# One projection of a split-precision decoder layer: both parts of h in one product, two PSUM pairs

## What is computed

```python
def even_mixer(h, w_in, lb, hg_norm_g, ret_norm_g, w_out):
    p = (h @ w_in).astype(jnp.float32)
    ...
    hq, hf, hi, hgate, rq, rk, rv, rgate = jnp.split(p, splits, axis=-1)
    f = lb + (1.0 - lb) * jax.nn.sigmoid(hf)
    o_hg = from_chunks(hgrn2_scan(to_chunks(jax.nn.silu(hq), HG_HEADS), to_chunks(1.0 - f, HG_HEADS),
                                  to_chunks(jnp.log(f), HG_HEADS), to_chunks(hi, HG_HEADS)))
```

## Time and profile before

| | |
|---|---|
| median of three executions | 895.02 us |
| the profiled execution | 895.32 us |
| its span (first to last instruction) | 893.5 us |
| outside the span | 1.8 us |
| TensorE busy | 884.4 us, 99% |
| VectorE busy | 652.2 us, 73% |
| ScalarE busy | 498.4 us, 56% |
| weights read | 159.73 MB on the SyncE queue |

### The profile page before, as it was taken

The page is one execution under the profiler, slowest core; times in us unless marked ns, Lnnn a source line. Parts: engine busy times, 40 slices in busy tenths (PEclk is TensorE's granted clock), DMA queues, the critical chain, the costliest instruction groups (busy, mean ns, idle before and its releaser), DMA issues.

```text
span 893.5 us, 13339 instructions
## 1 busy us (share of the span) xinstructions
PE 884.4 (99%) x5610; PEld 756.6 (85%) x5610; DVE 652.2 (73%) x790; ACT 498.4 (56%) x676; POOL 31.1 (3%) x25
## 2 busy tenths in 40 slices
PE   8999999999999999999999999999999999999997
PEld 7889888888888888888888888888879998888885
DVE  6999656569777767699567977777668895556655
ACT  6875556465444454766566544445558774366624
POOL 0000000000000000000000000000000083000000
PEclk9999999999999999999999999999999999999999
DMA  9644444466666664544336666666336344324431
GB/s 357 275 146 179 149 142 142 142 247 222 241 227 240 230 241 167 202 157 161 120 142 255 228 240 230 239 239 235 142 132 244 120 142 143 116 101 155 137 129 47
DMA packets 24155, 165.40 MB, mean 185 GB/s; under 512 B 2688, under 2 KB 2944, under 8 KB 4896
## 3 DMA queue, kind: packets, MB, share of 16 engines
q1 hardware_dynamic: 22608, 159.73, 48.9%
q0 software_dynamic: 1056, 4.34, 1.3%
q10 hardware_dynamic: 432, 0.49, 0.2%
HBM read 163.50 MB, written 1.05 MB: 184 GB/s over the span
## 4 chain that ended last, share of the span: by engine, by line
PE 91%; DVE 5%; ACT 2%; DMA 1%; issue 1%; DVEq 0%; SPq 0%; ACTq 0%
PE acc L633 30%; PE lin L594 11%; PE lin L615 6%; PE lin L622 6%; PE lin L599 6%; PE lin L616 6%; PE lin L573 3%; PE lin L581 3%; PE lin L574 3%; DVE w_lo L1889 2%; PE acc L841 1%; PE acc L725 1%; PE acc L726 1%; DVE arena L2342 1%; PE acc L735 1%; PE lin L678 1%
## 5 line engine op out<-in xcount | busy, mean ns | idle before, releaser
L1889 DVE TENSOR_TENSOR w_lo<-raw,w_hi 128x2048 fp32r<-128x2048 f32 x137 | 318.4, 2336 | 127.7 <-ACT w_hi L1384 127.1
L1384 ACT CAST w_hi<-raw 128x2048 fp32r<-128x2048 f32 x137 | 259.6, 1907 | 138.0 <-DMA raw<-in_weights 86.0
L633 PE MATMUL acc<-w_hi,f_hi 128*128 128x512 f32 x288 | 113.1, 393 | 0.0
L633 PE MATMUL acc<-w_hi,f_lo 128*128 128x512 f32 x288 | 112.4, 390 | 0.0
L615 PE MATMUL lin<-w_hi,h_both 128*128 128x512 f32 x272 | 109.4, 402 | 0.2
L594 PE MATMUL lin<-h_both,w_hi 128*128 128x512 f32 x448 | 106.7, 390 | 0.0
L616 PE MATMUL lin<-w_hi,h_both 128*128 128x512 f32 x272 | 106.3, 391 | 0.0
L594 PEld LDWEIGHTS lin<-h_both,w_hi 128*128 128x128 f32 x448 | 83.2, 188 | 16.7
L633 PE MATMUL acc<-w_lo,f_hi 128*128 128x512 f32 x288 | 78.9, 389 | 0.0
L622 PE MATMUL lin<-w_lo,h_both 128*128 128x512 f32 x272 | 68.1, 390 | 0.2 <-DVE w_lo L1889 0.2
L573 PE MATMUL lin<-h_both,w_hi 128*128 128x256 f32 x272 | 67.3, 287 | 0.0
(11 more groups left out here) (372 smaller groups left out, 1225.7 us busy)
## 6 DMA issues: line engine op xcount, KB each, us to landing
raw<-in_weights SPq DMA_DIRECT2D x149, 1024.0 KB, 4.8
rowbuf<-in_rows POOLq DMA_DIRECT2D x6, 512.0 KB, 4.0
x<-in_x_in SPq DMA_DIRECT2D x2, 512.0 KB, 4.5
raw<-in_weights SPq DMA_DIRECT2D x2, 512.0 KB, 7.3
arena<-in_const_even POOLq DMA_DIRECT2D x1, 1024.0 KB, 11.6
out<-x SPq DMA_DIRECT2D x3, 256.0 KB, 2.1
cst<-in_const SPq DMA_DIRECT2D x1, 580.0 KB, 10.4
out<-x ACTq DMA_DIRECT2D x1, 256.0 KB, 2.1
```

The costliest lines, as they stand in the source:

```text
L633: return pe.matmul(acc[:, at:at + 512], part_of(2 * j + k)[i][:, t * P:(t + 1) * P], w[:, k * 1024 + c * 512:k * 1024 + (c + 1) * 512], st ...
L1384: act.copy(w_hi[:, o % SPLIT, :], raw[:, j % RAW, :]).then_inc(hi_done, 1)
L1889: dve.tensor_tensor(w_lo[:, j % RAW, :], r, hi.bitcast(F32), ALU.subtract).then_inc(tile_split, 1)
```

## The change

hq's projection uses `project_both_parts` for each of its two tiles. The names `hq.0` and `hq.1` take two places in the list of pairs where `hq` had one. ScalarE copies the h_lo half of each pair to `cross(j)`; VectorE adds the h_hi half to it, into the halves of `qs`. The multiplication by 1/rms is then done on `qs` in SBUF, and Silu waits for a semaphore of its own.

```diff
--- before.py
+++ after.py
@@ -123,7 +123,7 @@
 
 
 def plan_lin():
-    g = ["hf", "hq", "hi", "hg", "rq", "rk", "rv0", "rv1", "rg0", "*y0a", "rg1", "*y0b", "*y0c"]
+    g = ["hf", "hq.0", "hq.1", "hi", "hg", "rq", "rk", "rv0", "rv1", "rg0", "*y0a", "rg1", "*y0b", "*y0c"]
 
     def mlp(l):
         out = [f"n{l}c0", f"n{l}c1"]
@@ -324,6 +324,7 @@
         x_r_turned = sem("x_r_turned")
         z0_ready = sem("z0_ready")
         qs_ready = sem("qs_ready")
+        q_scaled = sem("q_scaled")
         turns_ready = sem("turns_ready")
         h_lo_done = sem("h_lo_done")
         warm_ready = sem("warm_ready")
@@ -957,7 +958,8 @@
 
             first_projection("hf")
             project_feature_major("hf", (1,), first_r)
-            project_feature_major("hq")
+            project_both_parts("hq", 0)
+            project_both_parts("hq", 1)
             pe.wait_ge(s_const, 16)
             project_token_major("hi", (0,))
             level_scores(0)
@@ -1583,8 +1585,11 @@
             split_until(LAST["hf"] + 2)
             after(f_gate_ready)
             act.activation(ev("D"), ev("Z0"), ACT.Ln).then_inc(logf_ready, 1)
-            split_until(LAST["hq"] + 2)
-            read_out(act, "hq")
+            for j in range(2):
+                act.wait_ge(tile_used, ORDINAL[FIRST["hq"] + j] + 1)
+                act.copy(cross(j), part_of_pair(f"hq.{j}", 1)).then_inc(cross_read, 1)
+                split_until(LAST["hq"] + 1 + j)
+            after(q_scaled)
             act.activation(ev("qs"), ev("qs"), ACT.Silu).then_inc(qs_ready, 1)
             ahead("hq")
 
@@ -2095,6 +2100,11 @@
             def by_head(ap):
                 return ap.rearrange("p (h t) -> p h t", h=4)
 
+            def q_half(j):
+                after(cross_read)
+                dve.tensor_tensor(ev("qs", 512, j * 512).rearrange("p (b t) -> p b t", b=2), part_of_pair(f"hq.{j}", 0), cross(j),
+                                  ALU.add).then_inc(freed(f"hq.{j}"), 1)
+
             after(x_r_turned)
             link(dve.tensor_copy(ev("rv", T), acc[:, 1024:1024 + T]))
             split_until(LAST["hf"] + 1)
@@ -2110,6 +2120,7 @@
             dve.tensor_scalar(ev("k"), ev("Z0"), -1.0, 1.0, ALU.mult, ALU.add).then_inc(z_ready, 1)
             dve.wait_ge(s_const, 16)
             split_until(LAST["hf"] + 2)
+            q_half(0)
             after(logf_ready)
             for h in range(H):
                 ins = dve.tensor_tensor_scan(ev("b", T, h * T), const_of("reset"), ev("D", T, h * T), 0.0, ALU.mult, ALU.add)
@@ -2178,8 +2189,10 @@
             dve.wait_ge(s_even, 32)
 
             diffs(1)
-            filled(dve, "hq")
-            dve.tensor_tensor(by_head(ev("qs")), by_head(pair("hq")[:, :]), every, ALU.mult).then_inc(freed("hq"), 1)
+            q_half(1)
+            for j in range(2):
+                read_out(dve, f"hq.{j}")
+            dve.tensor_tensor(by_head(ev("qs")), by_head(ev("qs")), every, ALU.mult).then_inc(q_scaled, 1)
             split_until(LAST["hq"] + 3)
             after(qs_ready)
```

## The result

The changed kernel takes 896.45 us, the median of 20 executions (896.23 to 896.76, one at 898.3); the kernel before takes 895.09 (20 executions, 894.90 to 895.48). The ratio is 1.0016, with a 95% interval of 1.0010 to 1.0022. The change makes the kernel 1.36 us slower, 0.16%. The forecast was 896.6, with 1.57 us as its sum.

What follows compares the result with a forecast made beforehand. TensorE's queue bounds the kernel, with no slack against VectorE at tile 4's low part. VectorE's terms, 0.43 + 0.60 - 0.25 + 0.68 + 0.11 = 1.57 us, on the median 895.02 give 896.6 us; range 895.4 to 897.4.

Steps and rivals of the forecast that it cites:

- Rival 1: At tile 4, VectorE is not what TensorE waits for; the 0.44 us gain stays, 894.6 us; chance 0.08.
- The saving on TensorE: hq's two tiles on TensorE each get 0.22 us shorter, 0.44 in all, with 0.35 as the other end.
- The first sum: On VectorE after tile 3's low part: waiting for ScalarE's first copy costs 0.43 us, the addition itself 0.60.
- The second sum and the gap behind it: On VectorE ahead of the 1/rms product: the addition adds 0.68 us and the gap to its reader 0.11.
- The wait given back: VectorE's old wait for TensorE ahead of hq's product disappears, starting 0.25 us after its free place; returns 0.25 us.
- TensorE's wait: Ahead of the low products of hi's first tile, TensorE waits 2.0 us more for tile 4's low part.
- level 0 on TensorE: Silu ends at 37.2 us, level 0 is not reached before 39.8: delay hidden with 2.6 us to spare.
- The exponential of level 1: On ScalarE it ends at 41.4 us, VectorE wants it at 42.2: hidden by 0.8 us.
- rival 4: TensorE's two later 0.2 us waits could close, partly returning the delay: 896.2 us at best; chance counted within the forecast's 0.80.
- sign of being wrong: After tile 4, everything runs 1.6 us later to the end; a different shift at 45 us and at the end would refute this.
- Rival 2: ScalarE's second copy could hold VectorE's second sum, costing TensorE 0.85 us more: 897.4 us; chance 0.08.
- Rival 3, the clock: The 2 us TensorE stall at tile 4 lowers the granted clock, costing 2.2 us more: 898.8 us; chance 0.04.

Runs made afterwards that it cites:

- before_extra_ahead: Kernel before plus one unread 1024-column product on VectorE ahead of tile 4's low part: 896.77 us against 895.32, 1.45 slower.
- before_extra_behind: Kernel before plus the same unread 1024-column product on VectorE, placed between the low parts of tiles 4 and 5: 895.47 us against 895.33.
- after_again: The changed kernel, unaltered, run once more beside the kernel before: 896.70 us against 895.11, 1.59 slower.
- sum0_late: The changed kernel with VectorE's first sum moved behind the cumulative sums: 896.37 us against 895.32 for the kernel before, 1.05 slower.
- q_first: The changed kernel with tile 4's low part and all VectorE work for q ahead of the cumulative sums: 894.83 us against 895.32 for the kernel before.
- before_q_first: Kernel before with tile 4's low part and hq's product moved ahead of the cumulative sums on VectorE: 895.18 us against 895.33, 0.15 faster.
- before_extra3_ahead: Kernel before plus three unread 1024-column products on VectorE ahead of tile 4's low part: 900.30 us against 895.33, 4.97 slower.
- before_again: The kernel before, unaltered, run once more for a second trace: 895.00 us.
- low4_first: The changed kernel with tile 4's low part directly behind VectorE's first sum: median 898.65 us of five executions, 1.0032 times the kernel before.
- low4_again: The changed kernel with tile 4's low part directly behind the first sum, run again: six executions 896.81 to 897.24 us, four 898.50 to 898.82.

## Why the prediction was right

**The mechanism.** The forecast said that VectorE and TensorE arrive together at the low part of tile 4 and that the change's work on VectorE stands ahead of it. The new trace has that wait at that line. One reading was wrong: I took the 0.2 us of L622 in the earlier trace rows for the wait at 36.4 us, and it is another one, at 661 us. At 36.4 only the weight load had waited (0.28). The row of before behind that entry is this:

```profile
660.99 1.19 PE L622 MATMUL lin<-w_lo,h_both 128*128 128x512 f32 x4 [0.19 <-DVE w_lo L1889]
```

The argument stood on the timelines and not on that entry, so the sum was not touched. The pair before_extra_ahead and before_extra_behind shows the mechanism without any other part of the change. Rival 1 (gain stays, nothing lost) falls with the new trace: the extra on VectorE is not under 0.1 us but 1.55. The saving on TensorE is real, 0.40 us by the rows and 0.34 by the two q-first runs, and it is lost in the wait, as forecast.

One distance within each trace gives most of the measured differences to within 0.1 us: from the start of hq's last low products to the start of the scores of level 0. In the first trace of before it is 38.40 - 30.77 = 7.63 us, with this row at its end:

```profile
38.40 1.15 PE L955 MATMUL acc<-arena 128*64 128x64 f32 x32
```

| kernel | distance, us | more than before | less 0.40 where the products are wide | measured difference |
|---|---|---|---|---|
| the changed one | 9.37 | 1.74 | 1.34 | 1.36 |
| after_again | 9.40 | 1.77 | 1.37 | 1.59 |
| sum0_late | 9.05 | 1.42 | 1.02 | 1.05 |
| q_first | 7.48 | -0.15 | -0.55 | -0.49 |
| before_q_first | 7.48 | -0.15 | -0.15 | -0.15 |
| before_extra_ahead | 8.78 | 1.15 | 1.15 | 1.45, with 0.25 waited at 177 us |
| before_extra_behind | 7.64 | 0.01 | 0.01 | 0.14, with 0.24 waited at 177 us |
| before_extra3_ahead | 12.62 | 4.99 | 4.99 | 4.97 |

**The terms.** The sum was 0.43 + 0.60 - 0.25 + 0.68 + 0.11 = 1.57. In the new trace, from tile 3's low part:
- The first sum starts 28.96 - 26.34 = 2.62 us after it, where the cumulative sums started 2.20 after it: 0.42 for 0.43.
- It occupies 0.61 (28.96 to 29.57): 0.60.
- The second sum and the gap behind it take 34.03 - 33.24 = 0.79: 0.68 + 0.11.
- The product of 1024 columns in SBUF occupies 1.14 (34.03 to 35.17), as before.
- The wait given back is the one soft term. I took 0.25 from the first trace of before; in the second it is 0.45 (from 31.79 + 0.61 = 32.40 to 32.85). With that the sum is 1.37, and the two measured slowdowns are 1.36 and 1.59. Their intervals, 0.9 to 2.0 and 0.6 to 2.3 us, hold this sum and the one on record alike, so it is the rows that tell them apart and not the times. What I had as a constant is how long VectorE waits there for TensorE: 0.18 us in the first trace of before and 0.38 in four others (before_again and the three kernels with additional products), so my trace was the odd one.

That soft term is the one that was mis-sized: it is 0.25 to 0.45 us, and I should have kept both ends. TensorE's wait shows the same. I had 2.0 us for it. In low4_first, whose hq starts at the same time and where nothing is waited for at this place, the low products start at 35.75; in the changed kernel they start at 37.51, so the wait delays them by 1.76.

**What was hidden.** Silu started at 36.01 and ended at 37.07, and level 0 on TensorE starts at 39.5: hidden, as forecast. The exponential of level 1 ended at 41.24 and VectorE took it at 41.78: hidden by 0.5, where I had 0.8. Nothing was given back later (rival 4): the second wait for a low part in the list, 0.2 us at 661 and 662 us, stands in both kernels, and so do TensorE's two waits of 0.2 us for ScalarE. I had named as a sign of being wrong a shift at 45 us that differs from the shift at the end. Between the two first traces it is 1.15 us at the scores of level 1 (46.30 against 45.15) and 1.0 for the span. The two traces of one kernel, before, drift apart by more (0.03 us at 45, 0.3 for the span), so that sign can't be read here to 0.1 us.

**Rival 2** (the hand-over costs more) did not come: the second copy ended at 32.30 + 0.59 = 32.89 and the second sum started at 33.24, not held by it.

**Rival 3, the clock,** had a chance of 0.04 and was priced at 2.2 us. In 20 executions of the changed kernel one stands at 898.3, 1.9 us above the median, and none of the ten later ones does. Its mean granted clock is 0.998, which ordinary executions of that kernel have too, so it is open whether the clock was its cause. For a wait of 2.2 us (low4_first, low4_again) 7 of 15 executions are in the upper group, and for one of 3.3 us all five are slow. So the rival is real, and with the wait of the change it is rare at most. My argument against it was too strong: from the end of the kernel, where the clock fell over 4 us after the last product, I took a wait of half that length to be safe. The price came out at 1.6 to 2 us.

## What to carry to other kernels

Before adding work to an engine with slack on average, find where it meets the bound engine next, and read the two times there: this VectorE is busy 73% of the span and had none at 36 us. When such work must be added, order it by who waits for it: here the same instructions cost 1.4 us or, by the medians, save 0.4 to 0.5, by whether the cumulative sums, for which nobody waits yet, stand ahead of the weights' low part or behind it. And a long stall of TensorE can cost more than its length: here one of 3.3 us cost about 1.6 us more in all five executions, and with one of 2.2 us 7 of 15 executions were 1.6 to 2 us longer than the rest.

## What was not expected of the hardware

- The granted clock fell behind single waits of TensorE much shorter than the idle end of the kernel suggests: 3.26 us gave a stretch at 1.2 GHz in the profiled execution and by the times in all five, and 2.2 us gave two groups of times 1.6 to 2 us apart, the upper one with 7 of 15 executions. For the 2.2 us this rests on the times and the lower mean clock, not on a row. With a wait of 1.6 us one execution of 30 stood above the rest by that amount, and nothing shows that the clock was its cause.
- The start of a given instruction differs between executions before any of the edits comes into play: VectorE's low part of tile 3 started between 26.34 and 26.85 us in the 13 traces. A difference of a few tenths between two traces can only be read from distances within each.
